# GpSimd normalises the softmax probabilities in the two "four" layers of a six-layer hybrid network

## The reference

```python
s = jnp.einsum("bqhd,bkhd->bhqk", qi, k).astype(jnp.float32) * scale
s = jnp.where(kpos[None, :] <= qpos[:, None], s, -jnp.inf)
pr = jax.nn.softmax(s, axis=-1).astype(v.dtype)
return jnp.einsum("bhqk,bkhd->bqhd", pr, v)
```

## Time and profile before

| | |
|---|---|
| median of 3 runs | 2136.45 us (2135.91 to 2140.04) |
| the profiled execution, its own time | 2137.8 us |
| its span, first to last instruction | 2136.1 us |
| mean granted TensorE clock | 0.993 of full speed |
| busy: PE, DVE, ACT, POOL | 2077.8, 1488.5, 891.5, 177.8 us |
| the stretch of heads and tails, layer 4 | 1542.88 to 1565.50 us |
| the same stretch, layer 5 | 1882.40 to 1905.00 us |

### The profile page before, as it was taken

One profiled execution on the slowest core, in us unless ns is written; L12 is line 12 of the kernel. 1 busy time (PEld: TensorE's weight loads), 2 busy tenths in 40 slices (PEclk: granted clock), 3 DMA queues, 4 the chain that ended last, 5 costly groups with the idle time before them and its releaser, 6 DMA issues.

```text
span 2136.1 us, 35611 instructions
## 1 busy us (share of the span) xinstructions
PE 2077.8 (97%) x14377; PEld 1805.2 (85%) x14377; DVE 1488.5 (70%) x1941; ACT 891.5 (42%) x1174; POOL 177.8 (8%) x152
## 2 busy tenths in 40 slices
PE   7999999999999999999899999999989999999999
PEld 7988888798888798888798878887869998778998
DVE  5957754778854677744696685456688877588887
ACT  2254444334434423444323454445554334663332
POOL 5720000000000000000063300000100000100000
PEclk9999999999999999999999999999999999999999
DMA  7511655553555553555464046554325555414552
GB/s 227 178 61 61 205 189 191 170 190 99 180 196 182 173 178 119 197 192 182 139 180 155 3 149 216 186 186 154 103 78 171 186 183 170 138 50 158 194 180 99
DMA packets 267625, 333.81 MB, mean 156 GB/s; under 512 B 20562, under 2 KB 230613, under 8 KB 267493
## 3 DMA queue, kind: packets, MB, share of 16 engines
q1 hardware_dynamic: 267493, 331.93, 47.8%
HBM read 330.84 MB, written 1.05 MB: 155 GB/s over the span
## 4 chain that ended last, share of the span: by engine, by line
PE 86%; DVE 8%; ACT 3%; issue 2%; SPq 1%; DMA 0%; DVEq 0%; ACTq 0%
PE bank L586 45%; PE bank L554 29%; PE bank L1056 2%; DVE w_lo L2225 1%; ACT stat L1579 1%; PE bank L820 1%; PE bank L637 1%; DVE sq L2184 1%; PE bank L912 1%; PE bank L982 1%; PE bank L1137 1%; DVE pj L2184 1%; PE bank L926 1%; DVE xt L2184 1%; ACT w_hi L1624 1%
## 5 line engine op out<-in xcount | busy, mean ns | idle before, releaser
L2225 DVE TENSOR_TENSOR w_lo<-ring,w_hi 128x2048 fp32r<-128x2048 f32 (+2 forms) x289 | 615.2, 2131 | 375.3 <-ACT w_hi L1624 372.9
L1624 ACT ACTIVATE w_hi<-ring 128x2048 fp32r<-128x2048 f32 (+1 forms) x220 | 418.9, 1905 | 472.6 <-PE bank L586 287.3
L586 PE MATMUL bank<-w_lo,xh 128*128 128x512 f32 x992 | 267.7, 393 | 0.0
L554 PE MATMUL bank<-xh,w_hi 128*128 128x256 f32 x1752 | 239.9, 290 | 5.8 <-DVE w_hi L2223 5.0
L554 PE MATMUL bank<-xh,w_lo 128*128 128x256 f32 (+2 forms) x1832 | 242.4, 285 | 0.0
L586 PE MATMUL bank<-w_hi,xl 128*128 128x512 f32 x896 | 240.6, 390 | 1.0 <-DVE xl L2174 0.9
L586 PE MATMUL bank<-w_hi,xh 128*128 128x512 f32 x896 | 240.9, 391 | 0.6 <-ACT xh L1579 0.6
L554 PEld LDWEIGHTS bank<-xh,w_hi 128*128 128x128 f32 x1752 | 225.0, 195 | 15.8 <-issue 10.2
L554 PEld LDWEIGHTS bank<-xh,w_lo 128*128 128x128 f32 (+2 forms) x1832 | 229.1, 191 | 1.3
L554 PE MATMUL bank<-xl,w_hi 128*128 128x256 f32 x1752 | 230.1, 284 | 0.0
L554 PEld LDWEIGHTS bank<-xl,w_hi 128*128 128x128 f32 x1752 | 219.2, 192 | 0.4
(11 more groups left out here) (323 smaller groups left out, 2406.0 us busy)
## 6 DMA issues: line engine op xcount, KB each, us to landing
ring<-in_ffn_w_in_dram SPq DMA_DIRECT2D x264, 512.0 KB, 4.4
ring<-in_ffn_w_down_dram SPq DMA_DIRECT2D x88, 512.0 KB, 4.1
ring<-in_gdn_w_in_dram SPq DMA_DIRECT2D x64, 512.0 KB, 5.0
ring<-in_ffn_w_out_dram SPq DMA_DIRECT2D x44, 512.0 KB, 3.9
ring<-in_w_in_dram SPq DMA_DIRECT2D x40, 512.0 KB, 4.7
ring<-in_hgrn_w_in_dram SPq DMA_DIRECT2D x32, 512.0 KB, 4.5
ring<-in_gla_w_in_dram SPq DMA_DIRECT2D x24, 512.0 KB, 4.6
ring<-in_gdn_w_out_dram SPq DMA_DIRECT2D x16, 512.0 KB, 4.5
```

Of the source, the lines that this page charges most:

```text
L554: m = nc.tensor.matmul(cols, *((wk, xk) if tokens == ALL else (xk, wk)), start=(first and step == 0 and k == 0 and (j % 2 == 0)), stop=(la ...
L586: m = nc.tensor.matmul(bank[:, 0:width], xin[:, k0 + k, rows_of], w[:, k, c * width:(c + 1) * width], start=(first and step == 0 and k == ...
L1624: nc.scalar.activation(taken(high_part(u), u), taken(ring[:, u % RING, :], u), ACT.Copy).then_inc(*act_hi.tick())
L2225: v.tensor_tensor(w_lo[:, u % RING, 0:share], w[:, 0:share], high[:, 0:share], ALU.subtract).then_inc(*dve_lo.tick())
```

## The change

The two multiplications of each of the 8 heads go from DVE's list to POOL's, in both "four" layers. DVE marks its reciprocal as "reciprocal" (a signal of `dve_four`), POOL waits for it, multiplies the 128 columns of the first block and the 256 columns of the others by the two reciprocals of the head, and signals "normalised" on `pool_four`. PE waits for that signal in place of DVE's. Formats and values are the same; all other instructions keep their order.

```diff
@@ PE, step n, head n - 3
                         b = psum.claim(pe, "probs", layer, n)
-                        pe.wait_ge(*dve_four.at("normalised", layer, n))
+                        pe.wait_ge(*pool_four.at("normalised", layer, n))
@@ POOL
                 if kind == "four":
                     cosines(layer)
+                    for n in range(8):
+                        pool.wait_ge(*dve_four.at("reciprocal", layer, n))
+                        p = prob(n)
+                        g.tensor_scalar(p[:, 0:HALF], p[:, 0:HALF], small[:, n, 2:3], None, ALU.mult).then_inc(*pool_four.tick())
+                        g.tensor_scalar(p[:, HALF:TRI], p[:, HALF:TRI], small[:, n, 3:4], None, ALU.mult)\
+                            .then_inc(*pool_four.tick("normalised", layer, n))
@@ DVE, step n, head n - 2
                         dve.wait_ge(*act_four.at("exp", layer, n))
-                        v.reciprocal(small[:, n, 2:4], small[:, n, 2:4]).then_inc(*s.tick())
-                        p = prob(n)
-                        dve.wait_ge(*s.now())
-                        ts(s, p[:, 0:HALF], p[:, 0:HALF], small[:, n, 2:3], ALU.mult)
-                        ts(s, p[:, HALF:TRI], p[:, HALF:TRI], small[:, n, 3:4], ALU.mult, None, None, "normalised", layer, n)
+                        v.reciprocal(small[:, n, 2:4], small[:, n, 2:4]).then_inc(*s.tick("reciprocal", layer, n))
```

## The result

| | before | after |
|---|---|---|
| median of 4 runs, side by side | 2136.94 us | 2148.49 us (2147.56 to 2149.43) |
| span of the profiled execution | 2136.1 us | 2147.7 us |
| stretch of heads and tails, layer 4 | 22.61 us | 28.88 us |
| the same, layer 5 | 22.61 us | 27.38 us |

The account below looks back on a forecast made before the run. Bound by PE's weight products, with a ring of four engines limiting the two stretches: DVE spared 4.6 us a layer, 4.0 lost to waits, holds and hand-over, leaving 2 x 0.6 = 1.2 us; median 2136.45 to 2135.3, range 2132.9 to 2139.8.

Parts of the forecast that it names:

- The walk: Start times followed head by head through layer 4's stretch: it ends 0.6 us sooner, the same in layer 5; chance 0.47.
- I take 0.29 + 0.40 = 0.69 us a pair: POOL's two multiplies of a head, on 128 and 256 columns, priced from its select at 0.84 ns a column.
- 1.09 a pair: Upper price of POOL's two multiplies of a head, from its two-input operation: 725 ns at 256 columns, about 0.36 at 128.
- Rival (a): POOL's multiplies slower than its select: at 1.09 us a pair 1.15 us a layer lost, 2138.8; chance 0.25.
- list of waits: PE's waits before a head's transposes in the kernel before: 1.44 us at head 2, 0.24 at head 4, 1.29 at head 6.
- it stayed at 1.00 through waits of 1.44 us: PE's granted clock in the two stretches before the change; only longer waits were thought able to lower it.
- (d): Rival: PE's clock falls behind longer waits, adding only to the slow end of the slower-POOL rival; no chance of its own.
- (b): Rival: DVE's log instructions hold POOL behind odd heads; head 6 taken 0.25 us later than before, 2137.0; chance 0.18.
- 4.02 us for 1536 columns: Earlier POOL operation beside DVE's 0.69 us subtraction, read as 2.6 to 2.8 ns a column with no hold on POOL.
- R6: Start of head 6's reciprocal on DVE in layer 4: 1561.26 forecast, 1562.07 before; PE to take the head 1.08 us later.
- charged 0.20 and 0.27: Delays while POOL runs: 0.20 us on DVE's maximum behind even heads, 0.27 on its second log instruction behind odd heads.
- 8.8 forecast: Least fall of DVE's busy time over both layers: 0.55 x 16 = 8.8 us.

Follow-up runs that it names:

- b1_awake: Kernel after, with 3, 2, 2 and 3 filler products on PE before the transposes of heads 0, 2, 4 and 6: 2144.20 us, ratio 1.0041.
- b2_narrow_awake: Kernel after, POOL multiplying only 32 columns of each block, with 1, 1 and 2 PE fillers before heads 0, 5 and 6: 2136.40 us, ratio 0.9999.
- a4_tt: Kernel after, with POOL multiplying by tensor_tensor with the reciprocal broadcast, in place of tensor_scalar: 2140.55 us, ratio 1.0020.
- b3_tt_awake: Kernel after, POOL multiplying by tensor_tensor with broadcast reciprocal, with 2, 1, 1 and 2 PE fillers before heads 0, 4, 5 and 6: 2139.05 us, ratio 1.0014.
- a3_const: Kernel after, with POOL multiplying by the constant 0.5 in place of the reciprocals in SBUF: 2144.98 us, one run.
- a5_narrow: Kernel after, with both POOL multiplies cut to 32 columns, most probabilities left unnormalised: 2139.62 us, ratio 1.0017.
- c3_late: Kernel after, but POOL multiplies heads 3 and 7 only, by tensor_tensor, and DVE keeps the other six: 2139.90 us, ratio 1.0016.
- c1_even: Kernel after, but POOL multiplies the even heads only and DVE the odd ones: 2147.34 us, ratio 1.0057.
- d1_beta: Kernel before, multiplies kept on DVE, with POOL making log beta as a two-input subtraction in DVE's place: 2135.71 us, ratio 1.0004.
- c2_odd: Kernel after, but POOL multiplies the odd heads only and DVE the even ones: 2141.61 us, ratio 1.0028.

## Why the prediction was wrong

**The sum of the loss.** For both layers: the stretches went from 45.22 to 56.26, so +11.04. Of it the clock is 56.26 - 50.70 (b1_awake) = 5.56. The hand-over's price, from 0.69 to 1.50 us a pair at full clock, is 50.70 - 44.01 (b2_narrow_awake) = 6.69. The walk's own gain is 44.01 - 45.22 = -1.21. These differences take the fillers as harmless, which the waits left behind them, and PE's 0.15 us behind POOL before head 2, support. POOL's own holds behind DVE's log pair stand in both b1_awake and b2_narrow_awake, so they are in neither difference, but in the 44.01.

**The step that failed: "I take 0.29 + 0.40 = 0.69 us a pair".** It measured 1.50. The select of the earlier trace rows at 0.84 ns a column is no relative of the multiply. The trace of before had a hint of it, in two rows of the same groups as the earlier trace rows:

```profile
L1487 POOL MEMSET strict<- 128x384 f32 x1 | 0.4, 418 | 0.0
...
L1487 POOL MEMSET ones<- 128x128 f32 x1 | 0.2, 204 | 0.0
```

A memset reads no tensor and goes at the same 0.84 ns a column, while every POOL operation that reads two tensors takes 2.6 to 2.9. The multiply is near the latter: 0.36 us at 32 columns, 0.60 at 128 and 0.92 at 256 make about 2.5 ns a column on top of some 0.28. The upper bound, "1.09 a pair", taken from the two-input operation, was too low as well, so the truth lay outside both ends and the range could not reach it.

**Rival (a) was the right mechanism.** It put the turning point at 0.83 us a pair. Its two values (0.6 gained at 0.69, 1.15 lost at 1.09) make 4.4 us a layer for each us of pair. Carried on to 1.50 that is 2.9 us lost a layer; b1_awake shows 2.74. At a4_tt's 0.97 it is 0.6; a4_tt's layer 5 and b3_tt_awake show 0.59. At a3_const's 0.49 + 0.85 = 1.34 it is 2.2, and its layer 5 shows 1.54; its pair is also held less behind an odd head (0.29 us against 0.62), which the line doesn't have. So the line is rough, and its fit is in part luck, as rival (a) charged DVE 0.5 us for each held instruction, which DVE did not pay, and POOL nothing. The prediction's list of waits also leaves out the 0.68 us before head 0. That wait is on the path: it is where the longer hand-over shows first: PE takes head 0 1.02 us later than before.

**The step "it stayed at 1.00 through waits of 1.44 us" of (d) was read as a rule and is none.** The sum of the prediction has no term for the clock, and half of the loss in the stretches came through it. The clock also fell behind 1.14 us in a4_tt and 1.10 in a5_narrow, and in a5_narrow that happened with the predicted pair: the walk's own case would have lost to the clock the 1.5 to 1.7 us a layer that lie between a5_narrow and b2_narrow_awake. The kernel before has waits of 1.44 and 1.29 at clock 1.00, c3_late 1.43 and 1.54. In c1_even it stayed at 1.00 through 1.70, the wait behind which it fell in the kernel after, and in a3_const 1.53 and 1.52 went either way. So no length of a single wait decides it. What else does was not found.

**The step that rejected (b) failed too.** DVE's log pair holds POOL by 0.62 us behind the odd heads, in the kernel after, a5_narrow and b2_narrow_awake alike. The Trainium skill, "SBUF — State Buffer", section "Who interferes with whom", has the lock work both ways with the later engine blocked; the rows agree (POOL, 0.18 us later, goes from 0.60 to 1.22 us, while DVE keeps 0.54 and 0.55). The argument against it, 4.02 us for 1536 columns, compared two sizes of an operation that had not been seen free of DVE in that place. Behind R6 rival (b) had PE start 1.95 us later by its "R6 + 1.8" and the 0.15 to PE, and b2_narrow_awake shows 1.83 (the walk: 1.08); in b1_awake it is 2.58, of which 0.68 is the hold. This stands on the path before head 6. The walk's 22.0 us came out in spite of it by luck: DVE did not pay the 0.20 and the 0.27 charged before R2, nor the 0.27 behind R5, so R6 came 0.73 us sooner than the walk had it.

**The holds on DVE, charged 0.20 and 0.27.** They were too high: the maximum went from 0.17 to 0.28 once in the rows shown, with a mean of 184 ns over the 8 in the stretch against 169 before, and the log pair kept its length. DVE's busy time fell by 7.2 us on the page, less than the 8.8 forecast: the rows of merged multiplies overlap with their neighbours' (3.76 us a layer in the windows, so 0.47 a head rather than 0.55).

**What was right.** The place of the path, POOL's start (R + 0.25 against 0.24) and the waits of DVE for scores. That the end of the ring came out to 0.02 us at the prediction's own price is luck, as said. The chance of (a) beyond 0.2%, 0.11, was where the result fell, and further out than the range.

**Left open.** By their ratios the kernel after and all the variants with more than one run stand 1 to 5 us above what their stretches add. c1_even is the largest case: 12 us by its ratio, 7.5 in its two stretches; b1_awake has 8.8 by the medians and 5.5 in its stretches. The part between the two stretches shows where some of it lies (b2_narrow_awake, before, c1_even; columns as in the earlier trace rows):

```profile
1563.21:1878.60 315.39, 309.33 (x2061) 275.46 (x2061) 240.56 (x306) 141.81 (x165) 8.32 (x6) 0.99 0.49 160
1565.49:1882.46 316.97, 310.74 (x2061) 276.91 (x2061) 241.85 (x309) 141.82 (x165) 8.33 (x6) 0.99 0.49 159
1567.53:1886.08 318.55, 312.51 (x2061) 278.55 (x2061) 241.98 (x309) 141.33 (x163) 8.33 (x6) 0.98 0.49 159
```

The same 2061 products take 309.33, 310.74 and 312.51 us, and the part is longer by just that much. From 30 to 60 us behind the stretches the granted clock is 0.94 in both layers of the kernel before, b2_narrow_awake, b3_tt_awake and d1_beta, and 0.89 in both of the kernel after, a3_const, a4_tt, a5_narrow, c1_even, c2_odd and c3_late. The times of one kernel go with its clock as well: of 25 runs of the kernel before, the 11 with a mean clock of 0.994 average 2134.35 us and the 6 with 0.991 average 2138.69. So the clock has a part in the rest too, outside the stretches. How much of a median it makes can't be told from one profile of each kernel. Why the clock is lower there in most variants, and what lets it fall in one of two equal layers, is open.

## What to carry to other kernels

Work that is the last link before a waiting engine is not relieved by an idle engine that does it more slowly: its latency counts, not the busy time that it frees. Here the stretch got shorter at 0.69 us a pair and longer at 0.97, so the turning point is an estimated 0.83 us, and no form of the multiply was that quick. Where the trace has no row of the very operation on the very engine, the upper bound needs more room than the nearest relative gives, and the walk should be done at that bound before a chance is put on it. A wait that grows on PE should be charged twice, once for itself and once for a clock that may fall behind it; fillers that fit in the wait are the way to measure the second part, and one that is too long is itself the delay.

## What the runs showed of the hardware

- POOL's multiply by a scalar of a column is slower than its two-input multiply with the same column broadcast: 0.60 and 0.92 us against 0.40 and 0.61 at 128 and 256 columns. With a constant it is 0.53 and 0.85. The Trainium skill, "GPSIMD Engine Reference", section "4.1 Engine selection", calls one-input work on this engine roughly line-rate and advises VectorE for elementwise work; the advice held here, the rate did not: DVE does the 256 columns in 0.35 us.
- Held by DVE's pair of 0.54 and 0.55 us, POOL's tensor_scalar loses 0.62 us at its first instruction, whether that would take 0.36 or 0.60. Its tensor_tensor loses 0.23 and 0.31 us, at both instructions, and its tensor_scalar with a constant 0.23 and 0.06.
- The granted clock went to 0.50 and stayed there for up to 9.66 us in which PE was never idle, after a wait of 1.70 us in the kernel after; in c1_even the same wait left it at 1.00, and in a4_tt and a3_const it fell in one of two layers with the same waits.
